# Between attention and the long convolutions of a hybrid block: values between the turned Hyena tiles, difference and sum signalled singly, Fourier pieces one at a time

## The chip, the cores and the metric

The kernel runs on one core of a Trainium2 chip. The metric is the device time of one execution in microseconds (us). TensorE, VectorE, ScalarE and GpSimd stand in the profile as PE, DVE, ACT and POOL; SyncE (SP) issues the loads of the weights. All weights and inputs are f32.

## The reference, cut to what matters

Two layers of a diffusion backbone work on 256 latent and 256 context tokens of width 1024. In each layer four mixers read one projection of the normalised input: differential attention, Hyena, a 2-D Fourier mixer and a gated DeltaNet; their outputs are merged and an MLP follows. The last layer computes attention's queries, Hyena, Fourier and everything behind them for the latent stream alone.

```python
# differential attention, A_HEADS = 4
p = jax.nn.softmax(s, axis=-1)
a = p[:, :, 0] - lam * p[:, :, 1]
o = jnp.einsum('bhqk,bhkv->bhqv', a, v)
# Hyena: three parts of 512 channels, a short convolution, then twice:
u = centred_conv(pp[..., OFF_HY:OFF_FN], conv_w)
parts = jnp.split(u, HY_ORDER + 1, axis=-1)
z = parts[-1]
for n in range(HY_ORDER):
    z = parts[n] * long_conv(z, kf[:, n], bias[n])
# long_conv: irfft(rfft(z, 2L) * kf)[:L] + bias * z
# Fourier mixer: 4 groups of 128 channels, 256 tokens
y = jnp.fft.fft2(u, axes=(1, 3), norm='ortho').real
```

## The kernel before, in words

**Engines and semaphores.** Each engine runs its own hand-written program; the order in the code is the order of execution. TensorE's products go to eight PSUM banks of 128x512 f32. Four are *units* for the large products with weights. Four are *work* banks (`WORK = 4`), taken in turn by `fill(key)` for everything small: TensorE waits until the reader of the bank's last content has given it back (`give_fill`), and readers wait for the counter `filled`.

**Weights.** A *strip* of weights is loaded to `raw`, ScalarE casts it to fp32r (`split_hi`, L1286), and GpSimd or VectorE takes the rest (`split_lo`, L1295); a product takes three fp32r instructions (`mm3`, L578). Two split strips are held at a time, so the split of strip n+2 waits for the products with strip n (`hi_ahead(n)`, `lo_ahead(n)`). Small products are plain f32 (`mm`, L573), which the profile shows as two instructions each.

**Attention** (`att`). A unit of the inner loop is one head of one tile of 128 queries: 16 units in layer 0, 8 in layer 1 (the tiles are 4 and 2). TensorE computes the scores, VectorE the maximum, ScalarE the exponentials, VectorE `combine` (the difference of the two softmaxes, ending on L2078), TensorE transposes the result (`turned`, L688) and, once per tile, multiplies with the values (`values`: 16 products of 128x128 for four key tiles, 32 instructions in the profile). ScalarE's `o_copy` scales the values' result out of PSUM and takes the sums of squares for its norm.

**Hyena's projection** is woven into the same loop. `hy_pieces` multiplies 12 blocks of 128 channels; VectorE does the short convolution of each (`conv`, L2073 and L2078); TensorE transposes it to tokens by channels (`hy_turned`, L1059); ScalarE copies it (`u_copy`). Blocks 8 to 11 are the part `u2`, which is convolved; 0 to 3 and 4 to 7 are `u0` and `u1`, the gates. `hy_flip(li, j)` reverses the upper half of the tokens of part j by a product with a flipped identity (one product per stream).

**The long convolution** (`conv_forward`, `by_spectrum`, `conv_back`, `gated`). Layer 0 has two streams (s = 0, 1), layer 1 one. Order is n = 0, 1. VectorE forms the difference o and the sum e of the lower half and the flipped upper half (`even_odd`; what is made by the helper `tt` has L2069 in the profile). TensorE takes four products into four work banks: pieces fc 0 and 3 from e, 2 and 1 from o. VectorE multiplies by the filter's spectrum (12 operations of 128x512 per stream: products out of PSUM on L2517 and L2520, a difference and a sum of SBUF tiles on L2523 and L2069, each twice). TensorE transforms back into two banks (`anti`, copied by ScalarE, and `sym`), VectorE gates (L2534, L2537). GpSimd adds the bias to each order's spectrum (`add_bias`, L2775) before VectorE uses it.

**The Fourier mixer's projection** is eight pieces of 12 matmuls (`fn_piece`, two pieces to a strip, four strips), placed by hand in `hyena` to fill TensorE's waits. `attention_turned` transposes attention's normalised output, `fn_channels` and `fnet` do the transforms; ScalarE's DMA of `fn_table` comes behind the turned tiles. Then comes `merge`, a loop of large products.

Lines in the profile are those of the kernel before.

## Time and profile before

| | us |
|---|---|
| median of 3 runs | 2280.52 (2277.74 to 2284.1) |
| the profiled execution | 2286.33 |
| its span | 2284.3 |
| PE busy | 2159.3 (95%) |
| DVE busy | 1164.4 (51%) |
| ACT busy | 864.7 (38%) |
| POOL busy | 672.9 (29%) |
| mean granted clock of TensorE | 0.978 |

The span is from the first to the last instruction; the execution's own time is 2 us longer. Times inside are from the span's start. In a timeline row, start and duration are followed by engine, line, operation, tiles and the count of merged instructions; the duration of a TensorE row reaches to the modelled end of its last instruction, which lies beyond the start of the next row, and the idle time stands in brackets with what ended it. PEclk is the granted clock as a share of 2.4 GHz, a mean over the stretch. Layer 0's part around the change is at 684 to 757 us, layer 1's at 1858 to 1912 us.

### The profile page before, as it was taken

To read this page: it belongs to the slowest core of one execution; us is meant where nothing else is said; L and a number is where in the kernel's file an instruction comes from. 1 tells how busy PE (TensorE), PEld (TensorE's weight loads), DVE (VectorE), ACT (ScalarE), POOL (GpSimd) and SP (SyncE) were. 2 spreads that over 40 slices of the span, in tenths; PEclk is the share of its full clock that TensorE was granted. 3 is DMA by queue.
4 is the path that set the end of the run, shared out by engine and by line. 5 is a ranking of instruction groups with operands and counts; after the bars stand their busy time and mean duration, and the time that the engine had idled before them with its cause. 6 is when DMAs were issued, how large, how long until landed. Compare 5 with 4: busy or idle time off the path is not lost.

```text
span 2284.3 us, 35131 instructions
## 1 busy us (share of the span) xinstructions
PE 2159.3 (95%) x12612; PEld 1783.6 (78%) x12612; DVE 1164.4 (51%) x1935; ACT 864.7 (38%) x1673; POOL 672.9 (29%) x607
## 2 busy tenths in 40 slices
PE   7998999999998999999899999898999889998999
PEld 3555888887664888887788888677888778998999
DVE  3745454536557433335543443455455665556665
ACT  2234333242552332223322232354434454444443
POOL 2432222246212111015320123443334543114210
PEclk7999999999999999999999999999999999999999
DMA  7313233332652123233233332220001423554554
GB/s 234 133 62 114 86 106 111 111 103 83 203 180 81 47 92 101 92 101 93 74 95 99 95 98 95 85 74 20 20 20 57 134 80 119 173 179 132 186 179 148
DMA packets 225165, 245.27 MB, mean 107 GB/s; under 512 B 11475, under 2 KB 213652, under 8 KB 224020
## 3 DMA queue, kind: packets, MB, share of 16 engines
q1 hardware_dynamic: 221456, 232.19, 32.2%
q10 hardware_dynamic: 3588, 11.49, 1.4%
q8 instruction: 73, 1.20, 0.2%
q14 instruction: 48, 0.39, 0.1%
HBM read 237.36 MB, written 6.29 MB: 107 GB/s over the span
## 4 chain that ended last, share of the span: by engine, by line
PE 77%; DVE 10%; ACT 4%; issue 4%; POOL 3%; DMA 2%; ACTq 0%; DVEq 0%; POOLq 0%
PE psum L578 55%; PE psum L573 19%; DVE big L2069 5%; PE psum L688 2%; DVE big L2078 2%; POOL whl L1295 1%; ACT big L1509 1%; ACT tmp L1509 1%; ACT whl L1286 1%; DMA raw<-in_w_ada_dram 1%; POOL big L2680 1%; ACT big L1512 1%; DMA big<-in_hy_table_dram 0%; POOL big L1385 0%; DVE hhl L2199 0%
## 5 line engine op out<-in xcount | busy, mean ns | idle before, releaser
L578 PE MATMUL psum<-hhl,whl 128*128 128x512 f32 (+1 forms) x4416 | 832.5, 349 | 27.5 <-DVE hhl L2199 18.3
L578 PEld LDWEIGHTS psum<-hhl,whl 128*128 128x128 f32 x4416 | 705.8, 193 | 154.6 <-issue 45.1
L1286 ACT CAST whl<-raw 128x512 fp32r<-128x512 f32 x656 | 374.3, 618 | 872.8 <-PE psum L578 868.1
L1295 DVE TENSOR_TENSOR whl<-raw,whl 128x512 fp32r<-128x512 f32 x480 | 331.0, 731 | 488.0 <-ACT whl L1286 487.4
L573 PE MATMUL psum<-big 128*128 128x128 f32 (+6 forms) x2944 | 479.1, 326 | 37.5 <-DVE big L2069 14.5
L578 PE MATMUL psum<-bigr,whl 128*128 128x512 f32 (+1 forms) x2688 | 471.2, 337 | 4.2 <-DVEq L2599 2.5
L573 PEld LDWEIGHTS psum<-big 128*128 128x128 f32 (+2 forms) x2944 | 377.5, 194 | 115.3 <-issue 52.2
L578 PEld LDWEIGHTS psum<-bigr,whl 128*128 128x128 f32 x2688 | 415.6, 191 | 57.2 <-issue 4.9
L1295 POOL TENSOR_TENSOR whl<-raw,whl 128x512 fp32r<-128x512 f32 x176 | 229.8, 1327 | 396.5 <-ACT whl L1286 373.3
L1512 ACT COPY big<-psum 128x512 f32<-128x512 f32 (+2 forms) x324 | 180.3, 557 | 251.0 <-PE psum L573 168.4
L2069 DVE TENSOR_TENSOR big<-big,psum 128x512 f32<-128x512 f32 (+1 forms) x166 | 99.2, 598 | 147.2 <-PE psum L573 143.2
L2786 POOL TENSOR_TENSOR big<-big,tmp 128x512 f32<-128x512 f32 (+1 forms) x64 | 64.4, 1020 | 339.9 <-DVE tmp L2596 339.2
L578 PE MATMUL psum<-whl,hhl 128*128 128x512 f32 x672 | 157.4, 393 | 3.1 <-POOL whl L1295 3.0
L578 PEld LDWEIGHTS psum<-whl,hhl 128*128 128x128 f32 x672 | 125.2, 188 | 30.8 <-POOL whl L1295 4.7
L2759 POOL TENSOR_TENSOR big<-big,tab 128x512 f32<-128x512 f32 x48 | 61.0, 1270 | 264.5 <-ACT big L1512 233.7
L1347 POOL TENSOR_TENSOR tmp<-tmp 128x512 f32<-128x512 f32 (+1 forms) x32 | 28.7, 895 | 319.7 <-ACT tmp L1509 319.7
L688 PE MATMUL psum<-tab,big 128*128 128x128 f32 x528 | 81.4, 291 | 19.0 <-DVE big L2078 7.0
L688 PEld LDWEIGHTS psum<-tab,big 128*128 128x128 f32 x528 | 61.5, 148 | 42.7 <-issue 18.5
L2069 DVE TENSOR_TENSOR big<-big 128x512 f32<-128x512 f32 x80 | 67.8, 848 | 35.5 <-ACT big L1509 30.6
L2680 POOL TENSOR_SCALAR big<-xT,amp 128x256 f32<-128x256 f32 x48 | 54.2, 1141 | 39.8 <-issue 30.1
L2078 DVE SCALAR_TENSOR_TENSOR big<-psum,cols,big 128x510 f32<-128x510 f32 (+1 forms) x96 | 63.4, 660 | 3.4
L2073 DVE TENSOR_SCALAR big<-psum,cols 128x512 f32<-128x512 f32 (+1 forms) x48 | 31.8, 662 | 56.1 <-PE psum L578 40.9
(153 smaller groups left out, 1460.2 us busy)
## 6 DMA issues: line engine op xcount, KB each, us to landing
raw<-in_w_mlp_dram SPq DMA_DIRECT2D x128, 512.0 KB, 3.6
raw<-in_w_ada_dram SPq DMA_DIRECT2D x96, 512.0 KB, 4.7
raw<-in_w_in_dram SPq DMA_DIRECT2D x88, 512.0 KB, 3.5
raw<-in_w_gate_dram SPq DMA_DIRECT2D x64, 512.0 KB, 3.5
raw<-in_w_branch_dram SPq DMA_DIRECT2D x32, 512.0 KB, 3.4
raw<-in_w_o_dram SPq DMA_DIRECT2D x16, 512.0 KB, 3.4
hy_spectra<-big SPq DMA_DIRECT2D x2, 2560.0 KB, 8.5
big<-hy_spectra ACTq DMA_DIRECT2D x2, 1280.0 KB, 6.4
```

The lines of the kernel that those rows point to most:

```text
L573: return nc.tensor.matmul(o_, a, b, start=start, stop=stop)
L578: m = nc.tensor.matmul(o_, a(p_), b(q_), start=first and i == 0, stop=last and i == 2, skip_group_check=shared)
L688: m = nc.tensor.transpose(bank[:, i * P:(i + 1) * P], s, ids)
L1286: nc.scalar.copy(whl[:, r, 0, ks], raw_of(n)[:, ks]).then_inc(S["hi_ready"], 1)
L1295: ins = eng.tensor_tensor(whl[:, r, 1, ks], raw_of(n)[:, ks], whl[:, r, 0, ks].bitcast(F32), ALU.subtract)
L1509: return nc.scalar.activation(o_, i_, fn, **kw)
L1512: return nc.scalar.copy(o_, i_)
L2069: step(V.tensor_tensor(o_, a, b, op), s_)
L2078: step(V.scalar_tensor_tensor(o_, a, sc, b, op0, op1), s_)
L2680: ins = G.tensor_scalar(hn[:, k, sl], xT[:, k, sl], amp[:, li, which, k, s_:s_ + 1], None, ALU.mult)
L2759: step(G.tensor_tensor(hd(s_["dI"]), hd(s_["A"]), over_heads(const(f"off{32 << lv}")), ALU.mult), SD["aoff_ready"][d])
L2786: G.tensor_tensor(m_acc[:, i, tk], m_acc[:, i, tk], tmp[:, i % 2, tk], ALU.add)\
```

## The change

Four edits, all of order or of signals:

- `att`: in both layers the last tile's `values` come ahead of the transposes of Hyena block 11. In layer 0 flip 1 and flip 2 follow behind both. In layer 1 flip 1 goes ahead of block 10, and flip 2 moves to `hyena`, behind one Fourier piece. ScalarE's side follows: `o_copy` is parted into `o_scaled`, ahead of block 11's copy, and `o_squares`, behind the copies of flip 1.
- `even_odd`: the difference has a semaphore of its own (`odd_ready`). `conv_forward` takes the pieces in the order 2, 0, 1, 3 and waits for the difference before 2 and for the sum before 0.
- `by_spectrum`: instead of waiting for two pieces and then multiplying, VectorE waits for one, multiplies twice, gives the bank back, and takes the next; the order is 2, 0, then 1, 3.
- `hyena`: in layer 0 one Fourier piece stands behind each stream's forward convolution, one behind inverse 0 of order 0, one behind the turned attention, and two behind inverse 0 of order 1. In layer 1 the pieces are 1 + 3, then 1 behind the turned attention, and 3 behind the inverse convolution. ScalarE's casts and copies are reordered to match.

```diff
--- before.py
+++ after.py
@@ -356,7 +356,7 @@
         names = ("cols_ready cT_ready rstd_ready h_ready x_ready x_added gate_cols "
                  "g_ready decays_ready block_conv block_silu block_sq block_rstd block_normed block_tok "
                  "token_copied seg_ready o_normed y_turned stat_ready stat_root q_ready k_ready qkT_ready max_ready "
-                 "exp_ready a_ready aT_ready o_copied flipped eo_ready anti_ready hyk_ready hyf_clear hyf_arg hyf_sin hyf_cut hyf_sums hyf_taps z_ready zf_ready hy_u fn_u fn_v "
+                 "exp_ready a_ready aT_ready o_copied flipped odd_ready eo_ready anti_ready hyk_ready hyf_clear hyf_arg hyf_sin hyf_cut hyf_sums hyf_taps z_ready zf_ready hy_u fn_u fn_v "
                  "sg_ready mul_done acc_added relu_ready out_ready out_ready_dve out_stored hi_ready lo_ready modrow_ready "
                  "hn_dve hn_pool hhi_ready hyf_done yhi_ready ysplit acc_split wab_split sq_summed last_sq acc_hi xa_ready "
                  "gates_turned fn_odd mod_turned amp_ready inverse_ready").split()
@@ -1029,13 +1029,16 @@
                         turned(u - 1)
                 last = len(units) - 1
                 turned(last)
+                if li:
+                    hy_flip(li, 1)
                 hy_turned(li, 10)
                 if li == 0:
                     mod_turn(0, MODGROUPS - 1)
+                values(units[last][0], last)
                 hy_turned(li, 11)
-                hy_flip(li, 1)
-                values(units[last][0], last)
-                hy_flip(li, 2)
+                if li == 0:
+                    hy_flip(li, 1)
+                    hy_flip(li, 2)
 
             def hy_pieces(li, slot):
                 tk = toks(li)
@@ -1069,9 +1072,12 @@
 
             def conv_forward(li, n, s):
                 zz = hyz(li, n, s)
-                pe.wait_ge(S["eo_ready"], zz + 1)
                 e, o = HYB["u2"][:, 2 * s, :], HYB["odd"][:, s, :]
-                for fc, z in ((0, e), (2, o), (1, o), (3, e)):
+                for fc, z in ((2, o), (0, e), (1, o), (3, e)):
+                    if fc == 2:
+                        pe.wait_ge(S["odd_ready"], zz + 1)
+                    if fc == 0:
+                        pe.wait_ge(S["eo_ready"], zz + 1)
                     b = fill(("zf", zz, fc))
                     mm(b, wave(li, fc), z).then_inc(filled, 1)
 
@@ -1100,29 +1106,31 @@
                         fn_piece(li, next(pieces))
                 assert first_strip["fn", li] == n_strip[0] and first_unit["fn", li] == n_unit[0]
                 ss = list(streams(li))
+                if li:
+                    fn(1)
+                    hy_flip(li, 2)
                 for n in range(2):
                     for s in ss:
                         conv_forward(li, n, s)
-                        if n == 0 or li:
-                            fn(len(ss) if s == ss[-1] and li == 0 else 0)
+                        if li == 0:
+                            fn(1)
                     if li and n:
                         fn_channels(li)
                         fnet(li, range(2))
                     elif li:
-                        fn(4)
+                        fn(3)
                         attention_turned(li)
-                        fn(2)
-                    elif n:
-                        fn(2)
+                        fn(1)
                     for s in ss:
                         conv_back(li, n, s)
                         if li == 0:
-                            fn((2, 0, 2, 0)[2 * n + s])
+                            fn((1, 0, 2, 0)[2 * n + s])
                     if n == 0:
                         if li:
-                            fn(2)
+                            fn(3)
                         else:
                             attention_turned(li)
+                            fn(1)
                 if li:
                     fnet(li, range(2, HEADS))
                 else:
@@ -1847,6 +1855,10 @@
                     give_fill(act, ("aT", li, m_, h))
 
                 def o_copy(m_):
+                    o_scaled(m_)
+                    o_squares(m_)
+
+                def o_scaled(m_):
                     b = filled_bank(act, ("o", li, m_))
                     act.wait_ge(S["inverse_ready"], (0 if li == 0 else NT - 2) + m_ + 1)
                     for h in range(HEADS):
@@ -1854,6 +1866,8 @@
                                 scale=exp_inverse(m_, h))
                     step(ins, S["o_copied"])
                     give_fill(act, ("o", li, m_))
+
+                def o_squares(m_):
                     for h in range(HEADS):
                         ins = f(a_sq[:, 1, 0:P], a_o[:, m_, h * P:(h + 1) * P], ACT.Square,
                                 accum_out=small[:, O_STAT + 4 * m_ + h:O_STAT + 4 * m_ + h + 1])
@@ -1878,10 +1892,14 @@
                     if u:
                         probs_turned(u - 1)
                 probs_turned(len(units) - 1)
+                if li:
+                    flip_copy(li, 1)
                 u_copy(li, 10)
+                o_scaled(units[-1][0])
                 u_copy(li, 11)
-                flip_copy(li, 1)
-                o_copy(units[-1][0])
+                if li == 0:
+                    flip_copy(li, 1)
+                o_squares(units[-1][0])
                 stat_root(li, 3, sm(O_STAT, 16), P)
 
             def u_copy(li, blk):
@@ -1920,18 +1938,17 @@
                 if li:
                     hi_ahead(act, n0 + 1)
                     turned(li, "ya", ATT, subln)
-                    hi_ahead(act, n0 + 2)
                     fn_copy(li, 0)
                     fn_copy(li, 1)
                     anti_copy(li, 0, 1)
+                    hi_ahead(act, n0 + 2)
                 else:
                     anti_copy(li, 0, 0)
+                    anti_copy(li, 0, 1)
+                    turned(li, "ya", ATT, subln)
                     hi_ahead(act, n0 + 1)
                     fn_copy(li, 0)
                     fn_copy(li, 1)
-                    anti_copy(li, 0, 1)
-                if li == 0:
-                    turned(li, "ya", ATT, subln)
                 act.wait_ge(filled, fill_at["ya", li, NT - 1] + 1)
                 act.dma_start(fn_tab, fn_table).then_inc(fnw_loaded, 16)
                 if li == 0:
@@ -2503,7 +2520,7 @@
                     other = filled_bank(dve, ("flip", li, 2, s_))
                 else:
                     other = z[:, 2 * s_ + 1, :]
-                tt(o, z[:, 2 * s_, :], other, SUB)
+                tt(o, z[:, 2 * s_, :], other, SUB, S["odd_ready"])
                 tt(z[:, 2 * s_, :], z[:, 2 * s_, :], other, ADD, S["eo_ready"])
                 if n == 0:
                     give_fill(dve, ("flip", li, 2, s_))
@@ -2513,13 +2530,15 @@
                 z0, z1 = HYB["z0"][:, s_], HYB["z1"]
                 dve.wait_ge(S["hyk_ready"], 2 * li + n + 1)
                 for re, kr, ki, kr2 in ((0, 0, 2, 4), (1, 1, 3, 1)):
-                    br, bi = (filled_bank(dve, ("zf", zz, re)), filled_bank(dve, ("zf", zz, re + 2)))
-                    V.tensor_tensor(z0[:, re, :], br, spectrum(n, kr), MUL)
-                    tt(z0[:, re + 2, :], br, spectrum(n, ki), MUL)
-                    give_fill(dve, ("zf", zz, re))
-                    V.tensor_tensor(z1[:, 0, :], bi, spectrum(n, ki), MUL)
-                    tt(z1[:, 1, :], bi, spectrum(n, kr2), MUL)
-                    give_fill(dve, ("zf", zz, re + 2))
+                    for part in ((2, 0), (1, 3))[re]:
+                        b = filled_bank(dve, ("zf", zz, part))
+                        if part == re:
+                            V.tensor_tensor(z0[:, re, :], b, spectrum(n, kr), MUL)
+                            tt(z0[:, re + 2, :], b, spectrum(n, ki), MUL)
+                        else:
+                            V.tensor_tensor(z1[:, 0, :], b, spectrum(n, ki), MUL)
+                            tt(z1[:, 1, :], b, spectrum(n, kr2), MUL)
+                        give_fill(dve, ("zf", zz, part))
                     V.tensor_tensor(z0[:, re, :], z0[:, re, :], z1[:, 0, :], SUB)
                     tt(z0[:, re + 2, :], z0[:, re + 2, :], z1[:, 1, :], ADD, S["zf_ready"])
```

What the change does to TensorE's order. In layer 0, from the transposes of Hyena block 10 (L1059; 128x2 are the modulation's small products, 128x128 x16 the values, 128x512 the flips and the convolutions' products, L578 the Fourier pieces, 12 instructions each, L688 the turned attention). Before:

```order
L1059 MATMUL psum<-tab,big 128x128 x4
L573 MATMUL psum<-tab,rows 128x2 x2
L1059 MATMUL psum<-tab,big 128x128 x4
L573 MATMUL psum<-big 128x512 x2
L573 MATMUL psum<-big 128x128 x16
L573 MATMUL psum<-big 128x512 x10
L578 MATMUL psum<-hhl,whl 128x512 x24
L573 MATMUL psum<-big 128x512 x4
L578 MATMUL psum<-hhl,whl 128x512 x24
L573 MATMUL psum<-big 128x512 x4
L688 MATMUL psum<-tab,big 128x128 x16
```

And of the change, from the same place:

```order
L1062 MATMUL psum<-tab,big 128x128 x4
L573 MATMUL psum<-tab,rows 128x2 x2
L573 MATMUL psum<-big 128x128 x16
L1062 MATMUL psum<-tab,big 128x128 x4
L573 MATMUL psum<-big 128x512 x8
L578 MATMUL psum<-hhl,whl 128x512 x12
L573 MATMUL psum<-big 128x512 x4
L578 MATMUL psum<-hhl,whl 128x512 x12
L573 MATMUL psum<-big 128x512 x4
L578 MATMUL psum<-hhl,whl 128x512 x12
L573 MATMUL psum<-big 128x512 x4
L688 MATMUL psum<-tab,big 128x128 x16
```

The values stand ahead of block 11 (L1062 now), and the blocks of 24 are 12s between the groups of four products: forward 0, forward 1, inverse 0, inverse 1.

In layer 1, from the place where the loop over the units ends, before (`big,xT` are the products with tables that lie in `xT` there):

```order
L1059 MATMUL psum<-tab,big 128x128 x4
L573 MATMUL psum<-big,xT 128x512
L573 MATMUL psum<-big 128x128 x16
L573 MATMUL psum<-big,xT 128x512 x5
L578 MATMUL psum<-hhl,whl 128x256 x48
L688 MATMUL psum<-tab,big 128x128 x8
L578 MATMUL psum<-hhl,whl 128x256 x24
L573 MATMUL psum<-big,xT 128x512 x4
L578 MATMUL psum<-hhl,whl 128x256 x24
L573 MATMUL psum<-big,xT 128x512 x4
L573 MATMUL psum<-big 128x256 x16
```

And of the change:

```order
L573 MATMUL psum<-big,xT 128x512
L1062 MATMUL psum<-tab,big 128x128 x2
L573 MATMUL psum<-big 128x128 x16
L1062 MATMUL psum<-tab,big 128x128 x2
L578 MATMUL psum<-hhl,whl 128x256 x12
L573 MATMUL psum<-big,xT 128x512 x5
L578 MATMUL psum<-hhl,whl 128x256 x36
L688 MATMUL psum<-tab,big 128x128 x8
L578 MATMUL psum<-hhl,whl 128x256 x12
L573 MATMUL psum<-big,xT 128x512 x4
L578 MATMUL psum<-hhl,whl 128x256 x36
L573 MATMUL psum<-big,xT 128x512 x4
```

Flip 1 is ahead of block 10's transposes, the values are between the two blocks, a piece is ahead of flip 2 (the first of the five products), and the pieces are 1, 3, 1, 3 instead of 4, 2, 2.

## Rows read from the trace of the kernel before

**Rows 1.** The page: busy time, share of the span and instructions.
```profile
span 2284.3 us, 35131 instructions
...
PE 2159.3 (95%) x12612; PEld 1783.6 (78%) x12612; DVE 1164.4 (51%) x1935; ACT 864.7 (38%) x1673; POOL 672.9 (29%) x607
```

**Rows 2.** Timeline of PE, layer 0: start us, us, engine, instructions, [idle before, releaser].
```profile
686.50 0.66 PE L688 MATMUL psum<-tab,big 128*128 128x128 f32 x4 [1.85 <-DVE big L2078]
...
689.07 1.11 PE L1059 MATMUL psum<-tab,big 128*128 128x128 f32 x4 [1.13 <-DVE big L2078]
689.98 9.49 PE L573 MATMUL psum<-big 128*128 128x512 f32 x40
700.22 4.72 PE L573 MATMUL psum<-big 128*128 128x512 f32 x10 [0.75 <-DVE big L2069]
705.18 1.12 PE L573 MATMUL psum<-big 128*128 128x512 f32 x2 [0.25 <-DVEq L1266]
708.04 3.51 PE L573 MATMUL psum<-big 128*128 128x512 f32 x4 [1.73 <-DVEq L1266]
...
731.56 0.63 PE L688 MATMUL psum<-tab,big 128*128 128x128 f32 x4 [0.74 <-DVEq L1266]
...
739.88 1.13 PE L573 MATMUL psum<-big 128*128 128x512 f32 x2 [1.64 <-DVEq L1266]
...
747.76 3.59 PE L573 MATMUL psum<-big 128*128 128x512 f32 x8
...
756.64 10.50 PE L573 MATMUL psum<-big 128*128 128x512 f32 x40
```

**Rows 3.** Stretches of both layers: busy us by engine, PEclk, DMA share, GB/s.
```profile
core 0: us, PE busy (x) PEld busy (x) DVE busy (x) ACT busy (x) POOL busy (x), PEclk, DMA share, GB/s
684.00:690.00 6.00, 3.02 (x25) 2.70 (x22) 5.18 (x8) 2.46 (x5) 1.90 (x2) 0.82 0.50 156
690.00:700.00 10.00, 9.47 (x41) 6.08 (x40) 1.21 (x2) 3.79 (x12) 0.00 (x0) 0.77 0.20 65
700.00:712.00 12.00, 9.81 (x18) 3.69 (x19) 10.54 (x16) 1.25 (x6) 8.19 (x7) 0.86 0.32 111
728.00:745.00 17.00, 13.91 (x48) 7.22 (x47) 13.88 (x22) 3.83 (x6) 1.37 (x2) 1.00 0.21 70
1858.00:1876.00 18.00, 13.40 (x59) 9.16 (x57) 6.60 (x15) 7.56 (x24) 4.57 (x4) 0.81 0.25 68
```

**Rows 4.** Timeline of DVE, layer 0.
```profile
702.35 0.69 DVE L2517 TENSOR_TENSOR big<-psum,big 128x512 f32<-128x512 f32 x1 [0.63 <-PE psum L573]
...
709.51 0.70 DVE L2523 TENSOR_TENSOR big<-big 128x512 f32<-128x512 f32 x1
710.13 1.75 DVE L2069 TENSOR_TENSOR big<-big 128x512 f32<-128x512 f32 x1
711.91 0.69 DVE L2517 TENSOR_TENSOR big<-psum,big 128x512 f32<-128x512 f32 x1
...
730.07 0.69 DVE L2534 TENSOR_TENSOR big<-psum,big 128x512 f32<-128x512 f32 x1 [4.30 <-PE psum L688]
```

**Rows 5.** Timeline of POOL, layer 0.
```profile
707.17 4.16 POOL L2775 TENSOR_TENSOR big<-big,tmp 128x512 f32<-128x512 f32 x3 [1.72 <-DMA big<-hy_spectra]
```

**Rows 6.** Timeline of PE, layer 1.
```profile
1859.61 0.66 PE L688 MATMUL psum<-tab,big 128*128 128x128 f32 x4 [0.58 <-DVE big L2078]
1861.37 0.44 PE L1059 MATMUL psum<-tab,big 128*128 128x128 f32 x2 [1.11 <-DVE big L2078]
1863.11 0.69 PE L1059 MATMUL psum<-tab,big 128*128 128x128 f32 x2 [1.30 <-DVE big L2078]
...
1865.30 5.45 PE L573 MATMUL psum<-big 128*128 128x128 f32 x32
...
1873.18 3.70 PE L573 MATMUL psum<-big,xT 128*128 128x512 f32 x8 [1.57 <-DVE big L2069]
...
1882.47 1.03 PE L688 MATMUL psum<-tab,big 128*128 128x128 f32 x8
...
1894.30 3.70 PE L573 MATMUL psum<-big,xT 128*128 128x512 f32 x8 [1.59 <-DVE big L2069]
1897.84 7.07 PE L573 MATMUL psum<-big 128*128 128x256 f32 x32
```

**Rows 7.** Layer 1: a POOL split, the Fourier table's issue (ACT), DMA landing times.
```profile
1880.61 2.55 POOL L1295 TENSOR_TENSOR whl<-raw,whl 128x512 fp32r<-128x512 f32 x2 [4.16 <-ACT whl L1286]
...
1889.72 0.34 ACTq L1936 DMA_DIRECT2D big<-in_fn_table_dram  x1
...
big<-in_fn_table_dram ACTq DMA_DIRECT2D x2, 640.0 KB, 3.9
```

## The prediction

> **What bounds the kernel now.** I read the page first: TensorE is busy for 95% of a span of 2284.3 us, and no other engine is above 51% [rows 1]. So an edit pays only where TensorE stands still, or runs below its 2.4 GHz, at the places it touches. These are two stretches of TensorE's timeline, one in each layer, between attention and the last inverse product of the long convolutions.
>
> Layer 0 [rows 2]: after the transpose of Hyena block 10 TensorE is idle for 1.13 us before that of block 11 (started at 689.07), then 0.75 before the first forward convolution (700.22), 0.25 and 1.73 in the middle of the second one's four products, 0.74 before the last turned attention tile (731.56), then 0.15, 0.25, 1.64 and 0.31 among the forward products of order 1 (I show the 1.64). That is 7.0 us of visible idle time. Two costs lie beside it. A wait costs about 0.27 more than its idle column says: a pair of f32 instructions alone takes 1.13 us (739.88), in a stream the eight of a convolution take 3.59, so 0.43 each and 0.86 the pair. And the granted clock is 0.82 from 684 to 690, 0.77 from 690 to 700 and 0.86 from 700 to 712 [rows 3]. Since only two levels exist, those shares say that 2.2 + 4.6 + 3.4 us were spent at 1.2 GHz. Both falls follow idle time (1.85 us before 686.50, 1.73 before 708.04).
>
> I check this against the whole stretch. From 687.9 (the modulation's small products are over) to 756.64 are 68.7 us. The work in it at full rate: block 11's transposes 0.45; four flips at 0.86, 3.4; the values, 32 instructions, 3.6; sixteen forward products, 13.8; three inverse convolutions at 3.43, 10.3; sixteen transposes of attention, 1.75; eight Fourier pieces. Two pieces lie between the starts 747.76 and 756.64 with one inverse convolution, so a piece is (8.88 - 3.43) / 2 = 2.7, eight are 21.8. Sum 55.1; the excess is **13.6 us**. It is what can be won here.
>
> Layer 1 [rows 6]: idle 1.11 and 1.30 before the transposes of blocks 10 and 11 (1861.37, 1863.11), 1.57 before the forward convolution of order 0 (1873.18) and 1.59 before that of order 1 (1894.30), and a clock of 0.81 from 1858 to 1876 [rows 3], that is 6.8 us at 1.2 GHz: 32 instructions of values take 5.45 us there. From 1860.05 (the last transpose of probabilities is out) to 1897.84 are 37.8 us, with 29.2 of work (two flips 1.7, transposes 0.45, values 3.6, eight forward products 6.9, one inverse convolution 3.4, eight half-width pieces at 1.54, two turned tiles 0.9). Excess **8.6 us**.
>
> What TensorE waits for there is VectorE. Its spectrum product takes 9.56 us per stream (702.35 to 711.91, the second one starting right behind) [rows 4], while TensorE's four products and one Fourier piece take 3.43 + 2.7 = 6.1.
>
> **The change, part by part.** No instruction is added on any engine; only order and signals change.
>
> (1) Layer 0, values ahead of block 11. The values wait for the copy of the last probabilities, done on ScalarE at about 687.8, so they start at 687.9 and fill the 1.13 idle, during which VectorE finishes block 11 (689.0). The clock has already fallen, because the 1.85 idle before 686.50 stays. How long it stays low is unknown: between 0.0 (it does not fall) and the 6.8 us seen here. The fall at 708 was followed by work alone and lasted 3.4; after this change, too, only work follows, so I take 3.4, an excess of 1.6. Then 687.9 + 3.6 + 1.6 + 0.45 + 3.43 for the flips: forward products from 697.1 instead of 700.2. What this puts at risk: on ScalarE the scaling of the values (1.15 us, taken ahead of block 11's copy) delays that copy to about 695, and the second flips wait for it; they are ready at 695.2, so it is covered by the first flips.
>
> (2) The difference signalled alone. The product of the odd sine part needs only the difference, so TensorE starts one VectorE operation (0.72) before the sum is there: the idle 0.75 goes to about 0.1. In layer 1 both similar waits (1.57, 1.59) lose 0.7.
>
> (3) Spectrum product by pieces. VectorE takes each PSUM piece as it comes and gives it back after its two multiplications. It does the same work and saves only the first 0.9 of waiting.
>
> (4) Fourier pieces one at a time, which matters most in layer 0. Step by step, VectorE: difference and sum for two streams 696.3 to 699.2; spectrum products as before, 19.2, to 718.4; meanwhile TensorE does four products, a piece, four products (waiting 0.6 for banks), a piece, waits 1.7 for the bank of its inverse product, convolves stream 0 back (to 715.3), a piece, and is at stream 1 at 718.4, just as VectorE is. Stream 1 is back at 721.8, when VectorE is still gating stream 0 (4.3 us, to 722.7). So its 4.30 us of idle time at 730.07 [rows 4] vanishes. TensorE waits 1.6 for the last turned tile (the bank VectorE still reads), a piece, four products, a piece, four products, a piece (739.7), 1.3 for a bank, inverse 0, two pieces: the last inverse convolution starts at 750.3 instead of 756.64. Layer 0: **-6.3 us**. In terms of excess: 13.6 goes to 0.1 + 0.6 + 1.7 + 1.6 + 1.3 + 1.6 of clock = 6.9, about the same.
>
> (5) Layer 1. Flip 1 goes ahead of block 10, which fills 0.9 of its wait (0.45 stays); values start at 1861.6, behind the probabilities' copy. TensorE's idle time between 1858 and 1865 is halved, and I take the clock as staying up, which is 2.8 us (half of the 6.8 less the 1.30 idle in it). Bounds: 0 and 2.8. Block 11's transposes at 1865.2, one piece, flip 2 at 1867.0, then 1.0 of waiting for the difference, forward products at 1868.9 against 1873.2. Before order 1 stand three pieces (4.6 us) instead of two, so the 1.59 is gone: 1887.4 against 1894.30. **-6.9 us**, of which I give back 0.4, below.
>
> Covered and costed at nothing: GpSimd's split of the third Fourier strip (2.55 us from 1880.61, [rows 7]) is done just in time for the piece behind the turned tiles (1882.47 [rows 6]); from the end of piece 1 it has two pieces and these tiles to hide behind, as now. The Fourier table is issued at about 1886 instead of 1889.72, needed at 1890.9 instead of 1897.84; half its kind land within 3.9 us [rows 7], leaving 1. If that cover goes, each us of lateness is one us.
>
> GpSimd's own work now falls elsewhere in VectorE's. The one sum of a spectrum product that ran during the bias addition (707.17 to 711.33 on GpSimd) took 1.75 us against 0.69 for its neighbours [rows 4, 5]. In layer 0 as in layer 1 I expect one such hit more or less on the path, -1 to +2 us in all, and take +0.4. The Trainium skill (SBUF — State Buffer, Who interferes with whom) has VectorE instructions with two SBUF inputs contend with GpSimd's reads; the row agrees, and the multiplications from PSUM beside it are not slowed.
>
> Sum: -6.3 - 6.9 + 0.4 = **-12.8 us**. Everything behind both stretches is TensorE at work, so it carries to the end. The profiled execution took 2286.33 us and would take 2273.5; the median of the runs shown is 2280.52, so I predict 2267.7, rounded to 2268. A difference of 0.3% (6.8 us) is about what a measurement can tell from none.
>
> **The rivals.**
> - *The clock gives nothing back.* It stays low for 6.8 us in layer 0 and falls in layer 1: 1.6 + 2.8 less, 2272.1. For it: in layer 1 the 0.58 idle before 1859.61 [rows 6] and 0.45 of the next wait remain. Chance 0.14.
> - *VectorE is the bound in layer 0.* Its work from the first difference to the last spectrum product is 2.9 + 4 x 9.56 + 2 x 4.3 = 50 of the 54 us that I leave it (696.3 to 750.3); three slowed operations more, or one late piece, and TensorE waits again at the last inverse convolution. Both layers then give 5 to 6 in all: 2275. Chance 0.13.
> - *The waits only move.* The new early products meet banks that VectorE frees at the old times, and only (1) and (2) count, 3 us: 2277. Against it: the 4.30 idle on VectorE shows that it isn't saturated. Chance 0.04.
> - *Slower.* Many short waits spread among the pieces keep TensorE at 1.2 GHz in layer 0, whose forward, inverse, turned and Fourier work there is 48 us at full rate. Each us of it done at half rate costs one more, so this decides from 12.8 us of work (26 us of slow clock) on; with half of it slow the time is 2280.5 - 12.8 + 24 = 2292. Against it: from 728 to 745 TensorE was busy 13.91 of 17 us, with four waits in a row, and the clock was 1.00 [rows 3]. Chance 0.03. The Trainium skill (TensorE: Matmul & The Clock Gate, A second HAM failure mode: psum-queue depth-cycling) describes such an oscillation from small idle times at PSUM banks; this row speaks against it here.
>
> **How the numbers follow.** Forecast 0.66, at 2263 to 2273 (clock bounds and hits by GpSimd). With the first two rivals at 2272.1 and 2275 and a median that wanders by some 2 us, the range is 2262 to 2277; it leaves out the last two rivals and a tail. Faster by over 0.3% means under 2273.7: 0.66, most of the first rival, a third of the second: 0.82. Within 0.3%: 0.15. Slower: 0.03.
>
> **What would show it.** Right: values directly behind the modulation's products; no idle above 1 us before the first forward products; VectorE's 4.30 gone; waits of 1 to 2 us before inverse convolutions and the last turned tile; clock near 1.00 in layer 1's stretch; the two stretches shorter by about 6 and 7. Wrong: the stretches shorter by these, yet the time is not; the clock below 0.9 anywhere between layer 0's pieces; a wait on the Fourier table.

## The result, and the profile after

The changed kernel takes 2270.11 us (median of 6 runs, 2267.55 to 2273.51) against 2282.93 (6 runs) for the kernel before: ratio 0.9948, 95% interval 0.9938 to 0.9959. That is 12.8 us, 0.56%, and under the 0.9970 that I called a measurable gain. Over all runs of this study the means are 2270.0 us (16 runs of the change) and 2283.2 (60 of before), 13.2 apart. The profiled execution took 2267.55 us. One run of the kernel e8 below took 2575.65 us at a granted clock of 0.785 and is left out of every median, mean and ratio.

The page of the changed kernel:

```profile
span 2265.7 us, 35133 instructions
...
PE 2149.3 (95%) x12612; PEld 1777.9 (78%) x12612; DVE 1163.2 (51%) x1935; ACT 864.2 (38%) x1673; POOL 672.0 (30%) x607
```

TensorE's work is the same 12612 instructions, and it is busy for 10 us less than before [rows 1]. The clock accounts for that: a mean of 0.978 over 2284 us is some 100 us at 1.2 GHz, 0.982 over 2266 us some 81, and work done there takes twice as long, so 19 us less of it give some 10 back. The rest of the 18.6 us between the two profiled spans is idle time.

TensorE's timeline in layer 0, the counterpart of [rows 2] (start us, us, instructions, [idle before, releaser]):

```profile
684.80 0.66 PE L688 MATMUL psum<-tab,big 128*128 128x128 f32 x4 [1.85 <-DVE big L2095]
...
685.73 0.51 PE L573 MATMUL psum<-tab,rows 128*128 128x2 f32 x4
686.22 3.81 PE L573 MATMUL psum<-big 128*128 128x128 f32 x32
689.87 0.60 PE L1062 MATMUL psum<-tab,big 128*128 128x128 f32 x4
690.31 7.37 PE L573 MATMUL psum<-big 128*128 128x512 f32 x16
697.11 3.33 PE L578 MATMUL psum<-hhl,whl 128*128 128x512 f32 x12
...
702.40 1.13 PE L573 MATMUL psum<-big 128*128 128x512 f32 x2 [0.25 <-DVEq L1274]
703.84 1.12 PE L573 MATMUL psum<-big 128*128 128x512 f32 x2 [0.31 <-DVEq L1274]
...
709.22 3.67 PE L573 MATMUL psum<-big 128*128 128x512 f32 x8 [1.49 <-issue]
...
722.00 0.63 PE L688 MATMUL psum<-tab,big 128*128 128x128 f32 x4 [1.62 <-DVEq L1274]
...
740.74 6.05 PE L578 MATMUL psum<-hhl,whl 128*128 128x512 f32 x24
746.63 10.50 PE L573 MATMUL psum<-big 128*128 128x512 f32 x40
```

The values (686.22) start right behind the modulation's products, block 11's transposes (689.87) no longer wait, and the 16 instructions at 690.31 are both flips and the first forward products in one run: the idle 0.75 is gone. The pieces of 12 (697.11) stand between the groups. What is left is 1.85 before the last probabilities, 0.25 and 0.31 in the second group, 1.49 before the first inverse product (this profile names no releaser; that of e12 names VectorE's hand-back of a bank for the same wait, 1.45) and 1.62 before the last turned tile. From the last probabilities to the last inverse convolution are 746.63 - 684.80 = **61.8 us, against 756.64 - 686.50 = 70.1** [rows 2].

The clock, the counterpart of [rows 3] (busy us by engine, PEclk, DMA share, GB/s):

```profile
core 0: us, PE busy (x) PEld busy (x) DVE busy (x) ACT busy (x) POOL busy (x), PEclk, DMA share, GB/s
682.00:688.00 6.00, 4.15 (x40) 3.57 (x33) 5.47 (x8) 2.75 (x6) 2.20 (x2) 1.00 0.42 137
688.00:698.00 10.00, 9.97 (x42) 5.57 (x41) 4.18 (x7) 5.03 (x17) 2.21 (x3) 1.00 0.33 103
698.00:710.00 12.00, 9.95 (x33) 5.76 (x32) 11.20 (x15) 1.14 (x2) 7.42 (x7) 1.00 0.21 88
726.00:743.00 17.00, 17.00 (x55) 10.11 (x54) 15.36 (x24) 3.39 (x7) 5.29 (x4) 1.00 0.23 75
1848.00:1866.00 18.00, 16.23 (x100) 11.92 (x99) 11.02 (x22) 8.69 (x25) 5.94 (x5) 1.00 0.39 133
684.80:746.63 61.83, 58.13 (x224) 36.83 (x225) 50.04 (x74) 15.19 (x34) 16.44 (x13) 1.00 0.25 83
1849.54:1880.46 30.92, 29.75 (x173) 22.08 (x174) 19.49 (x31) 13.98 (x36) 16.71 (x14) 1.00 0.38 127
```

The last two rows are the whole stretches: the clock never fell in either layer's stretch in this profile. In a second profile of the same kernel (e1) it did, over the values:

```profile
679.00:697.00 18.00, 16.12 (x86) 10.98 (x76) 9.92 (x16) 8.09 (x23) 4.77 (x5) 0.91 0.36 104
697.00:745.00 48.00, 44.29 (x157) 27.52 (x156) 43.09 (x62) 8.99 (x15) 14.66 (x11) 1.00 0.20 68
```

0.91 over 18 us is some 3 us at 1.2 GHz, and this profile's stretch is 63.5 us, 1.7 longer. A third one (e11) also has 63.4.

VectorE in layer 0, the counterpart of [rows 4]:

```profile
693.23 2.96 DVE L2086 TENSOR_TENSOR big<-big,psum 128x512 f32<-128x512 f32 x4 [5.28 <-PE psum L573]
...
704.54 1.77 DVE L2086 TENSOR_TENSOR big<-big 128x512 f32<-128x512 f32 x1
...
710.32 1.75 DVE L2086 TENSOR_TENSOR big<-big 128x512 f32<-128x512 f32 x1
...
726.36 0.69 DVE L2539 TENSOR_TENSOR big<-psum,big 128x512 f32<-128x512 f32 x1 [1.67 <-PE psum L573]
```

It starts 3.8 us earlier after the last probabilities than before (693.23 - 684.80 against 698.76 - 686.50), and from there to TensorE's last inverse convolution its longest wait is the 1.67 before order 1; the 4.30 is gone. Two sums with both inputs in SBUF take 1.77 and 1.75 us; GpSimd works beside both:

```profile
701.58 4.18 POOL L2794 TENSOR_TENSOR big<-big,tmp 128x512 f32<-128x512 f32 x3 [1.75 <-DMA big<-hy_spectra]
708.58 2.94 POOL L1303 TENSOR_TENSOR whl<-raw,whl 128x512 fp32r<-128x512 f32 x2 [2.83 <-ACT whl L1294]
```

TensorE in layer 1, the counterpart of [rows 6]:

```profile
1849.54 0.66 PE L688 MATMUL psum<-tab,big 128*128 128x128 f32 x4 [0.58 <-DVE big L2095]
...
1851.30 0.44 PE L1062 MATMUL psum<-tab,big 128*128 128x128 f32 x2 [0.25 <-DVE big L2095]
1851.59 3.81 PE L573 MATMUL psum<-big 128*128 128x128 f32 x32
...
1859.09 3.70 PE L573 MATMUL psum<-big,xT 128*128 128x512 f32 x8 [0.85 <-DVE big L2086]
...
1869.28 3.59 PE L573 MATMUL psum<-big,xT 128*128 128x512 f32 x8
...
1877.03 3.60 PE L573 MATMUL psum<-big,xT 128*128 128x512 f32 x8
1880.46 7.07 PE L573 MATMUL psum<-big 128*128 128x256 f32 x32
```

Waits of 1.11 and 1.30 have become 0.25 and none, 1.57 has become 0.85, the 1.59 before order 1 (1877.03 now) is gone. From the last probabilities to the first Fourier transform are 30.9 us, against 38.2.

So the stretches are 8.3 and 7.3 us shorter in this pair of profiles. The remaining 3 us of difference between the spans lie outside them, where nothing was changed. Ahead of layer 0's stretch are 1.7 (684.80 against 686.50), as much as a slow stretch that the profile before has and this one has not costs. The first row is before, the second the change:

```profile
655.00:670.00 15.00, 13.28 (x90) 9.09 (x89) 6.02 (x17) 5.95 (x13) 2.50 (x2) 0.89 0.54 176
655.00:670.00 15.00, 13.46 (x105) 10.18 (x103) 6.08 (x17) 6.13 (x14) 2.50 (x2) 1.00 0.58 186
```

0.89 over 15 us is 3.3 us at 1.2 GHz, half of it lost. Some 1.2 us behind layer 1's stretch stay unexplained. I take the median's 12.8 as the gain.

### The profile page after: what moved, and what is told of

Same layout as the page of the kernel before. It is cut to its first block, busy times and chain, and to the rows that moved or that the text cites. A ratio compares the mean times of both kernels' runs of the same rounds, so it can differ in the third digit from the quotient of the medians.

```text
span 2265.7 us, 35133 instructions
## 1 busy us (share of the span) xinstructions
PE 2149.3 (95%) x12612; PEld 1777.9 (78%) x12612; DVE 1163.2 (51%) x1935; ACT 864.2 (38%) x1673; POOL 672.0 (30%) x607
## 4 chain that ended last, share of the span: by engine, by line
PE 72%; DVE 9%; issue 9%; ACT 4%; POOL 4%; DMA 2%; ACTq 0%; DVEq 0%; POOLq 0%
PE psum L578 51%; PE psum L573 19%; DVE big L2086 5%; PE psum L688 2%; DVE big L2095 2%; POOL whl L1303 1%; ACT big L1517 1%; ACT tmp L1517 1%; POOL big L2805 1%; DMA raw<-in_w_ada_dram 1%; ACT whl L1294 1%; POOL big L2699 1%; ACT big L1520 1%; DMA big<-in_hy_table_dram 0%; POOL big L1393 0%
## 5 line engine op out<-in xcount | busy, mean ns | idle before, releaser
L578 PE MATMUL psum<-hhl,whl 128*128 128x512 f32 (+1 forms) x4416 | 832.4, 348 | 26.4 <-DVE hhl L2216 17.8
L578 PEld LDWEIGHTS psum<-hhl,whl 128*128 128x128 f32 x4416 | 704.6, 193 | 153.0 <-issue 45.0
L573 PE MATMUL psum<-big 128*128 128x128 f32 (+6 forms) x2944 | 472.1, 322 | 34.6 <-DVE big L2086 13.7
L578 PE MATMUL psum<-bigr,whl 128*128 128x512 f32 (+1 forms) x2688 | 470.0, 336 | 4.7 <-DVEq L2618 2.5
L578 PEld LDWEIGHTS psum<-bigr,whl 128*128 128x128 f32 x2688 | 414.3, 190 | 57.9 <-issue 4.7
L578 PE MATMUL psum<-whl,hhl 128*128 128x512 f32 x672 | 157.5, 393 | 3.1 <-POOL whl L1303 3.0
L578 PEld LDWEIGHTS psum<-whl,hhl 128*128 128x128 f32 x672 | 125.2, 188 | 30.9 <-POOL whl L1303 4.8
L688 PE MATMUL psum<-tab,big 128*128 128x128 f32 x528 | 81.5, 291 | 19.8 <-DVE big L2095 6.9
L688 PEld LDWEIGHTS psum<-tab,big 128*128 128x128 f32 x528 | 61.6, 148 | 43.3 <-issue 19.4
L2095 DVE SCALAR_TENSOR_TENSOR big<-psum,cols,big 128x510 f32<-128x510 f32 (+1 forms) x96 | 63.4, 660 | 3.4
```

The source lines that it names most:

```text
L573: return nc.tensor.matmul(o_, a, b, start=start, stop=stop)
L578: m = nc.tensor.matmul(o_, a(p_), b(q_), start=first and i == 0, stop=last and i == 2, skip_group_check=shared)
L688: m = nc.tensor.transpose(bank[:, i * P:(i + 1) * P], s, ids)
L2095: step(V.scalar_tensor_tensor(o_, a, sc, b, op0, op1), s_)
```

## The experiments

Each kernel was profiled once, the kernel before too, and timed in 5 to 12 runs beside the kernel before. Since the same two stretches are read in each, they stand in one table. Layer 0's runs from the transposes of the last probabilities to the last inverse convolution, layer 1's from these transposes to the first Fourier transform, the part between from the end of the one to the start of the other; the clock is the mean over the runs. The medians of before and of the change are those of all 60 runs and of the first 6.

| kernel | layer 0 us | layer 1 us | between us | median us | ratio to before (95%) | clock |
|---|---|---|---|---|---|---|
| before | 70.1 | 38.2 | 1103.0 | 2283.4 | | 0.979 |
| the change | 61.8 | 30.9 | 1102.9 | 2270.1 | 0.9948 (0.9938 to 0.9959) | 0.981 |
| e1, the change again | 63.5 | 30.9 | 1103.1 | 2268.3 | 0.9945 (0.9930 to 0.9960) | 0.982 |
| e2, weave undone | 69.1 | 30.9 | 1103.0 | 2276.3 | 0.9973 (0.9962 to 0.9983) | 0.980 |
| e3, hand-over undone | 64.6 | 37.1 | 1102.7 | 2279.6 | 0.9986 (0.9975 to 0.9996) | 0.978 |
| e4, signals undone | 64.3 | 32.6 | 1107.9 | 2274.9 | 0.9963 (0.9952 to 0.9973) | 0.980 |
| e5, weave alone | 66.1 | 38.2 | 1102.7 | 2280.7 | 0.9985 (0.9976 to 0.9994) | 0.979 |
| e6, 0.9 us of work added | 63.5 | 30.9 | 1103.4 | 2271.6 | 0.9941 (0.9926 to 0.9955) | 0.981 |
| e7, 1.8 us added | 63.4 | 30.9 | 1106.6 | 2271.0 | 0.9949 (0.9934 to 0.9964) | 0.981 |
| e8, taken further | 60.4 | 29.5 | 1107.2 | 2267.3 | 0.9931 (0.9916 to 0.9945) | 0.980 |
| e9, further and 1.8 us added | 60.4 | 29.5 | 1109.7 | 2271.4 | 0.9942 (0.9929 to 0.9956) | 0.980 |
| e10, e8's kernel again | 60.3 | 29.5 | 1103.1 | 2268.3 | 0.9936 (0.9922 to 0.9949) | 0.980 |
| e11, the change, third time | 63.4 | 30.9 | 1102.3 | 2269.4 | 0.9943 (0.9929 to 0.9956) | 0.982 |
| e12, pieces undone | 64.4 | 31.5 | 1102.5 | 2273.4 | 0.9953 (0.9938 to 0.9967) | 0.980 |

**The change again (e1, e11).** Expected of e1:

> The changed kernel itself, for a second profile and a shared chip. Theory: the two stretches (last transposes of probabilities in layer 0 to the last inverse convolution: 61.8 us in the profile of the change, 70.1 before; last transposes in layer 1 to the first Fourier transform: 30.9 against 38.2) are the same again to 0.3 us except where the granted clock falls in them; time 12 to 13 us under the kernel before. The rival: that the first profile was lucky with the clock, so that a fall shows in the stretch and it takes 63 or more.

and of e11:

> The changed kernel, on the same chip as the two kernels taken further. Both theories: 12 to 15 us under the kernel before; stretches 61.8 (63.5 where one slow stretch falls in) and 30.9.

Layer 1 is the same to 0.05 us. Layer 0 has 61.8 once and 63.5 and 63.4 in the other two, both with one slow stretch of the clock over the values. e6 and e7 below are the same kernel up to the end of this stretch, and have the slow stretch and 63.5 and 63.4 as well. So the rival holds: the first profile was the lucky one of five. The times agree.

**Weave undone (e2).** The kernel of the change with layer 0's pieces in the places of before, and ScalarE's order to match:

```diff
-                        if li == 0:
-                            fn(1)
+                        if n == 0 and s == ss[-1] and li == 0:
+                            fn(2)
...
+                    elif n:
+                        fn(2)
...
-                            fn((1, 0, 2, 0)[2 * n + s])
+                            fn((2, 0, 2, 0)[2 * n + s])
...
                             attention_turned(li)
-                            fn(1)
```

> The changed kernel with layer 0's Fourier pieces in the old places. Theory (step 4 as I priced it together with the hand-over): layer 0's stretch 3.5 to 4 us longer than with the change (65.5), layer 1's the same, time +3.7. Rival: the weave is the main gain of layer 0: +6 us. Other rival: the waits only move, and the weave gives under 1.5 us.

Layer 0 took 69.1 us: 7.3 over the lucky profile and 5.6 over the other two. The rival is nearer. Why my 3.7 was too little is in its stretches (columns as above):

```profile
684.00:700.00 16.00, 14.12 (x71) 10.02 (x68) 8.29 (x13) 7.54 (x22) 2.88 (x3) 0.89 0.33 101
700.00:712.00 12.00, 9.14 (x21) 4.24 (x20) 11.20 (x16) 0.00 (x0) 7.26 (x7) 0.86 0.31 106
712.00:730.00 18.00, 17.61 (x72) 12.02 (x71) 13.18 (x19) 6.14 (x11) 5.45 (x4) 1.00 0.15 48
730.00:745.00 15.00, 12.94 (x33) 6.18 (x33) 13.91 (x22) 1.13 (x2) 0.00 (x0) 0.89 0.17 59
```

and in two rows of its TensorE timeline:

```profile
705.68 1.13 PE L573 MATMUL psum<-big 128*128 128x512 f32 x2 [1.98 <-DVEq L1275]
...
737.68 3.51 PE L573 MATMUL psum<-big 128*128 128x512 f32 x4 [1.57 <-DVEq L1275]
```

VectorE's spectrum product is waited for again among the four products (1.98, 1.57), and behind each of these waits the clock falls: 0.86 from 700 to 712 and 0.89 from 730 to 745, beside the fall over the values that the change has as well. Two slow stretches of 3.3 us, half of each lost where they are filled with work, are up to 3.3 us, and the waits are the rest. I had priced the waits alone. By the ratios e2 takes 6.4 us more than e1, where 3.7 were expected.

**Hand-over undone (e3).** The order of before at the end of attention, in both layers:

```diff
-                if li:
-                    hy_flip(li, 1)
                 hy_turned(li, 10)
...
-                values(units[last][0], last)
                 hy_turned(li, 11)
-                if li == 0:
-                    hy_flip(li, 1)
-                    hy_flip(li, 2)
+                hy_flip(li, 1)
+                values(units[last][0], last)
+                hy_flip(li, 2)
```

with ScalarE's copies to match and layer 1's pieces at 4, 2, 2.

> The changed kernel with the old order at the end of attention in both layers (values behind the transposes of block 11 and flip 1, flip 2 at once, layer 1's pieces 4, 2, 2). Theory: layer 0's stretch +4 us, of it half from the clock that falls again at the two idle times, layer 1's +5.8 us, of it 2.8 from the clock; time +9.7. Rival (clock gives nothing): +2 and +3, time +5.

Layer 1: +6.1, as expected to 0.3. Its rows are those of before [rows 6] again, but for the two that the separate difference had already halved:

```profile
1856.41 0.44 PE L1059 MATMUL psum<-tab,big 128*128 128x128 f32 x2 [1.11 <-DVE big L2085]
1858.15 0.69 PE L1059 MATMUL psum<-tab,big 128*128 128x128 f32 x2 [1.30 <-DVE big L2085]
...
1867.33 3.70 PE L573 MATMUL psum<-big,xT 128*128 128x512 f32 x8 [0.85 <-DVE big L2076]
...
1888.17 3.70 PE L573 MATMUL psum<-big,xT 128*128 128x512 f32 x8 [0.86 <-DVE big L2076]
```

Layer 0: +2.7 over the lucky profile, +1.1 over the others, where I expected 4. Here only one slow stretch stood in it, as in those others, so the +1.1 is waits: 1.13 before block 11, 2.05 before the first inverse product and 1.10 before the last turned tile, against 1.49 and 1.62 in the change. Time +9 to +10 against 9.7 expected; the stretches give 7.2 to 8.8, so that agreement is partly luck.

**Signals undone (e4) and pieces undone (e12).** e4 puts back one signal, the order 0, 2, 1, 3, and two pieces at a time; e12 only the last:

```diff
-                    for part in ((2, 0), (1, 3))[re]:
-                        b = filled_bank(dve, ("zf", zz, part))
...
+                    br, bi = (filled_bank(dve, ("zf", zz, re)), filled_bank(dve, ("zf", zz, re + 2)))
```

> The changed kernel with one signal for difference and sum, pieces in the order 0, 2, 1, 3 and VectorE waiting for two pieces at a time. Theory: one VectorE operation (0.7 us) at each place where TensorE or VectorE stands waiting: layer 0's stretch +1.4, layer 1's +0.7; time +2.1. Rival: covered everywhere, since VectorE is busy and its queue only shifts: 0 to 0.5.

> The changed kernel with VectorE waiting for two pieces at a time again, the difference still signalled alone. Theory (step 3 of the prediction: saves only the first 0.9 of waiting in each spectrum product that starts on an idle VectorE): layer 0's stretch +0.8 us or less, layer 1's 0, time +0.8 at most. Rival (it carries most of what undoing both signals cost): layer 0 +0.8, layer 1 +1.7, time +3 or more.

Against the 63.4 us of the profiles with a slow stretch (both have one), layer 0 is 0.8 longer with both undone and 0.9 with the pieces alone: in layer 0 the pieces are what counts. In layer 1 it is 1.7 and 0.5: there the difference's own signal gives most. Two rows of e4's layer 1 (TensorE):

```profile
1870.99 3.70 PE L573 MATMUL psum<-big,xT 128*128 128x512 f32 x8 [1.57 <-DVE big L2083]
...
1883.36 1.98 PE L573 MATMUL psum<-big,xT 128*128 128x512 f32 x4 [0.15 <-DVE big L2083]
```

the first is the 1.57 of before, 0.85 with the change. The theory had the sum right (2.1 expected, 2.5 measured in the stretches) and gave the layers the wrong way round. In time e4 is 4 us over e1 by the ratios and 6 by the means, more than the stretches say; its own profile has more in the part between (1107.9), which no edit touches. For e12 the stretches are +1.5 (0.8 expected). Its mean is 2.7 us over e11's, but its interval overlaps the change's: the time doesn't tell.

**Weave alone (e5).** The kernel before with nothing but layer 0's new places for the pieces.

> The kernel before with layer 0's Fourier pieces placed as in the change, and nothing else of it. Theory (half of the gain is waits, half is the clock, and spreading the pieces saves both): layer 0's stretch 64 to 66 us against 70.1, layer 1's 38.2 as before, one slow stretch of the clock less in layer 0; time 4 to 5 under the kernel before. Rival (the weave pays only behind the earlier hand-over): under 2 us.

66.1 us against 70.1, layer 1 untouched, and 6.8 us at 1.2 GHz in layer 0 instead of 10.2: the weave pays without the hand-over. Time -3.4 by the ratio, a little under the 4 to 5 expected; its interval (1.4 to 5.5) doesn't exclude the rival's 2, the stretch does. Alone the weave gives 4.0, taken away last it costs 5.6 to 7.3. So the parts are not independent. In these profiles most of the difference is in the clock: e5 lacks one slow stretch of before, e2 has two that the change has not.

**Is the part behind fixed? (e6, e7, e9).** In e4 the part between the stretches, which no edit touches, took 5 us more, with slow stretches near 1505, 1546 and 1778. I asked whether a shift in time alone does this, by making some of the transposing products of Hyena's output twice:

```diff
-                    for h in range(HEADS):
+                    for h in list(range(HEADS)) * (2 if li == 0 and i < 1 else 1):
```

(`i < 2` in e7 and e9.)

> The changed kernel with four of the transposing products of Hyena's output in layer 0 made twice (0.9 us more of TensorE's work in a stretch where it never waits). Theory (what lies behind is shifted in time, and which of its idle times end in a slow clock changes with that): both stretches as in the change, but the time differs from +0.9 by up to 4 us either way, and the difference is found in slow-clock stretches of layer 1's DeltaNet part. Rival (the time behind is fixed): +0.9, within 1 us.

> The same with eight of them made twice: 1.8 us of added work. Theory: differs from +1.8 by up to 4 us and not by the same as the run with 0.9. Rival: +1.8, within 1 us.

> The kernel taken further, with 1.8 us of TensorE's work more (eight of the transposing products of Hyena's output in layer 0 made twice). Theory: in the ten profiles so far the part between the two stretches takes 1102.7 to 1103.4 us or 1106.6 to 1107.9, the second with three slow stretches near 1456, 1497 and 1538, and which of the two goes with where the work falls in time. The kernel taken further is in the long case; moved by 1.8 us it should leave it: 1103 + 1.8 in that part instead of 1107.2, and the time 2 us shorter in spite of the added work. Rival: the work is simply added, +1.8.

The theory falls in its form. Means over the runs are 2271.1 (e6) and 2271.4 (e7) against 2270.0 for the change: +1.1 and +1.4, with standard errors of 1.1 and 1.3, which fits the added work. The kernel taken further had 1107.2 in one profile and 1103.1 in the next (e8, e10), so the long and the short case come and go with one and the same kernel; and the shifted one (e9) stayed long and took 3.1 us more than e10, not 2 less. What decides between the two cases from run to run stays open.

**Taken further (e8, e10).** Edits on top of the change:

```diff
+                if li == 0:
+                    hy_turned(li, 10)
+                    hy_flip(li, 1)
                 turned(last)
...
-                values(units[last][0], last)
-                hy_turned(li, 11)
+                values(units[last][0], last, with_block=11)
+                hy_flip(li, 2)
...
+                        if with_block and h == 2:
+                            hy_turned(li, with_block, bh)
...
-                            attention_turned(li)
                             fn(1)
+                            attention_turned(li)
```

> The changed kernel taken further: block 11's transposes in the middle of the values, flip 1 and block 10 ahead of the last probabilities in layer 0, flip 2 ahead of the first Fourier piece in layer 1, and layer 0's fourth piece ahead of the turned attention. Theory: the 1.85 us idle ahead of the last probabilities and the 1.6 ahead of the last turned tile are filled, and layer 1's forward products start 1.3 earlier: layer 0's stretch, counted from the transposes before the last (682.3 in the change's profile), 3.2 us shorter, layer 1's 1.3 shorter; time -4.4. Rival (VectorE is the bound of layer 0): only -1.7 there, -3.0 in all.

> The kernel taken further, again, beside the change on the same chip. Theory: 2 to 3 us under the change in time (4.4 less of waits, 2 to 4 lost again to the clock behind). Rival: no difference.

TensorE in e10, from the last probabilities but one:

```profile
682.86 0.66 PE L688 MATMUL psum<-tab,big 128*128 128x128 f32 x4
683.39 0.63 PE L1067 MATMUL psum<-tab,big 128*128 128x128 f32 x4
683.86 1.88 PE L573 MATMUL psum<-big 128*128 128x512 f32 x4
685.58 0.60 PE L688 MATMUL psum<-tab,big 128*128 128x128 f32 x4
686.02 0.51 PE L573 MATMUL psum<-tab,rows 128*128 128x2 f32 x4
687.70 2.02 PE L573 MATMUL psum<-big 128*128 128x128 f32 x16 [1.18 <-ACT big L1524]
689.56 0.60 PE L1067 MATMUL psum<-tab,big 128*128 128x128 f32 x4
```

The 1.85 idle is filled by block 10 and flip 1, block 11 (689.56) stands in the middle of the values. But a new wait of 1.18 stands before the values: the probabilities' copy now comes behind two flips' copies on ScalarE. From 682.86 to the last inverse convolution at 745.90 are 63.0 us, against 64.3 in the change's first profile (682.29 to 746.63), so 1.3 less and not 3.2; layer 1 is 1.5 less (1.3 expected). In waits the rival's 1.7 and 3.0 are nearer than the theory's 3.2 and 4.4. Against e1, which had the slow stretch over the values, layer 0 is 3.0 shorter (66.0 from the same place), since none of the three profiles of this order (e8, e9, e10) had that slow stretch. In time, 2268.2 (mean of 10 runs) against 2270.0 (16): 1.8 less, with a standard error of 0.8. The mean clock over these runs is 0.980 against 0.982, some 4 us lost again elsewhere, as e10's theory had it. It beats the kernel before clearly and the change barely.

## Why the prediction was right

The time forecast was 2268 for a median of 2280.5 before, a gain of 12.8; measured are 12.8, and 13.2 over all runs. That the two agree to a tenth is luck: the forecast had 13.2 less in the two stretches, the profiles have 15.6 (the first) and 13.9 (e1), and medians of this kernel wander by 2 us; the kernel before had 2280.5 in three runs and 2283.4 in sixty. Its steps:

- **(1) Values ahead of block 11.** Right: they follow the modulation's products at once, and from the last probabilities to the first forward product (690.31 plus eight instructions of 0.43) it took 8.9 us, with 9.0 plus 1.6 of clock forecast. The 1.6 for one slow stretch was seen in four of five profiles (e1, e11, e6, e7: 63.4 to 63.5 against 61.8). The reason given, that the clock has already fallen because the 1.85 of idle time stays, is too strong: in the first profile the 1.85 is there and the clock stays at 1.00.
- **(2) The difference alone.** Right in layer 1 (1.57 to 0.85, and e4 shows it), and the first wait of layer 0 is gone.
- **(3) By pieces.** Right in size where it counts: e12 has 0.9 in layer 0. I hadn't expected its 0.5 in layer 1.
- **(4) The weave.** The schedule that I worked out is the one in the profile: waits of 0.6, 1.7, 1.6 and 1.3 forecast, 0.56, 1.49, 1.62 and none visible measured; VectorE's 4.30 gone. Layer 0's stretch: -6.3 forecast, -6.6 and -6.7 in two profiles, -8.3 in the one without a fall. The prediction's excess of 13.6 had the slow clock of the kernel before in it. My expectation for e2 had not: that is why taking the weave away costs 5.6 to 7.3 where I expected 3.7.
- **(5) Layer 1.** -6.9 forecast, -7.3 measured, the clock stayed up in all profiles with the new hand-over and fell again when it was undone (e3: 0.83 from 1846 to 1866).
- **GpSimd.** The 0.4 given back for slowed operations was not needed. The prediction counted the one sum beside the bias addition; the profile before has three of 1.75 to 1.76 us in layer 0's stretch (710.13, 719.79, 750.46), the other two beside GpSimd's weight splits, and the change has two (704.54, 710.32) and two differences of 1.09 and 1.19. Together the operations with two SBUF inputs lie 3.6 us above 0.69 each before and 3.1 after. The Trainium skill (SBUF — State Buffer, Who interferes with whom) has VectorE instructions with two SBUF inputs contend with GpSimd's reads, and those with at most one not. The trace agrees: the operations out of PSUM beside these stay at 0.69.
- **The Fourier table** and the third strip stayed covered: no wait stands before 1880.46 or before the piece behind the turned tiles.

How much was clock? In layer 0 the kernel before spent 10.2 us at 1.2 GHz [rows 3], 9.1 of them working, which is 4.5 lost; the change loses 1.7 or nothing. In layer 1 it is 2.8 against nothing. That is about 6 of the 13.9 us in the stretches of before and e1, and some 8 are waits: the forecast had 5.7 and 7.5. The kernel before was profiled once, and its share of clock in layer 0 can vary too: with the same hand-over, e5 had 6.8 us at 1.2 GHz over the values, as before, and e3 3.4. The runs say the same as the profiles: the mean clock is 0.9790 over the 54 runs of before beside the experiments and 0.9817 over the 16 of the change, which is some 6 us of 2275. The rival of a clock that gives nothing back is refuted by layer 1 and by the 3.4 us, not 6.8, that layer 0 spends at 1.2 GHz at most; the one of VectorE as the bound by its 1.67 of idle time and by a TensorE that doesn't wait from 722.39 to 746.63; the one of waits that only move by the stretches; the slower one by a clock of 1.00 from 726 to 743 with the pieces in between.

## What to carry to other kernels

List the idle times of the bounding engine in a stretch with their releasers, write its schedule out operation by operation with durations from the trace, and check the method on the kernel before. Here it gave three of the new order's four waits to some 0.2 us and layer 0's stretch to 0.4. The forecasts for single parts taken away or added, with too little slow clock in them or too much, were off by 2 to 3 us (e2, e3, e8). Filler work belongs one piece at a time behind each group that feeds the slower engine, and an independent product belongs ahead of the step that still waits for its input. Count the slow clock that can follow TensorE's waits of 1 to 2 us as part of their price, as a range: it was some two fifths of the gain, but the change's own waits of 1.49 and 1.62 us were followed by none.

## What the runs showed that I had not expected

- Two executions with the same waits ahead can differ in whether the clock falls behind them: the 1.85 us of idle time before the last probabilities was followed by a slow stretch in two of three profiles of one kernel, and in those of e6 and e7, at a cost of 1.7 us each. The same holds of a wait in the middle: 1.64 us was followed by a clock of 1.00 in the kernel before [rows 2, 3], 1.57 us by 0.89 in e2.
- The part between the two edited stretches took 1102.3 to 1103.4 us in ten profiles and 1106.6 to 1109.7 in four (e4, e7, e8, e9), with both cases for the same kernel (e8, e10). Of this e6, e7 and e9 have 0.9, 1.8 and 1.8 us of added work; no other edit touches it. All four long ones have three slow stretches some 41 us apart (1456, 1497 and 1538 in e7); e7 lacks the slow stretch between 1800 and 1831 that the others have, and is 1104.8 us without the added work. Differences of up to 5 us between two profiles of this kernel are therefore no evidence unless they are read in the stretch that was edited.
- The time of a run follows its mean granted clock: of the 12 runs of e2 the three at 0.978 took 2277.9 to 2280.2 us, the four at 0.981 took 2271.9 to 2272.5. 0.003 of 2275 us is 6.8, and the groups' means are 6.7 apart.
